# Two transformer blocks on one core: gate and MLA projections cut into pieces between attention steps, values in two passes with a fold, first stage reordered over four banks

## What is computed

```python
for l in range(DEPTH):
    xn = rms_norm(x, attn_norm[l])
    (nsa_q, kv_c, kv_s, kv_w, nsa_g, cq, ckv, k_rope_raw,
     gate_a, gate_b) = split_cols(xn @ w_in[l])
    o_a = nsa_attention(nsa_q, kv_c, kv_s, kv_w, nsa_g, cmp_pe[l], cmp_w1[l], cmp_w2[l], pos)
    o_b = mla_attention(cq, ckv, k_rope_raw, mla_q_norm[l], mla_kv_norm[l],
                        mla_w_uq[l], mla_w_ukv[l], pos)
    merged = (jax.nn.sigmoid(gate_a) * (o_a @ nsa_w_o[l])
              + jax.nn.sigmoid(gate_b) * (o_b @ mla_w_o[l]))
    x = x + merged @ w_out[l]
    hn = rms_norm(x, mlp_norm[l])
    x = x + jnp.square(jax.nn.relu(hn @ w_up[l])) @ w_down[l]
return rms_norm(x, final_norm)
```

## Time and profile before

| | |
|---|---|
| timed executions | 1684.75, 1685.53 and 1688.5 us; median 1685.53 us |
| span of the profiled execution, first to last instruction | 1683.2 us |
| busy share of the span, by engine | PE 94%, PE weight loads 77%, DVE 58%, ACT 40%, POOL 23% |
| mean granted TensorE clock | 0.974 of full speed |

### The profile page before, as it was taken

How to read it: one execution, slowest core, us unless ns; L and a number is a source line. 1 busy time by engine, 2 the same in 40 slices (tenths; PEclk the granted TensorE clock), 3 DMA queues, 4 the chain that set the end, 5 groups by cost and what they waited for, 6 DMA issues and landing times.

```text
span 1683.2 us, 23737 instructions
## 1 busy us (share of the span) xinstructions
PE 1587.0 (94%) x7742; PEld 1302.3 (77%) x7742; DVE 968.4 (58%) x1514; ACT 669.9 (40%) x1233; POOL 382.6 (23%) x410
## 2 busy tenths in 40 slices
PE   6899999889999999999998999999899999999996
PEld 4678878777778888888877888777678788888885
DVE  6765668775664343434566656777756544434346
ACT  5244447664342221322333552776623322222232
POOL 3660024343001010101056400434520000001010
PEclk9999889989999999999999998999999999999998
DMA  4234410002423233232223443000053222323232
GB/s 159 94 125 144 152 45 14 14 26 90 143 83 109 90 100 100 87 100 100 91 87 111 134 154 103 26 14 26 14 170 105 82 100 94 100 89 102 96 98 102
DMA packets 43238, 154.51 MB, mean 92 GB/s; under 512 B 5280, under 2 KB 5280, under 8 KB 43136
## 3 DMA queue, kind: packets, MB, share of 16 engines
q1 hardware_dynamic: 37152, 133.19, 23.9%
q0 software_dynamic: 5408, 17.95, 3.0%
q10 hardware_dynamic: 576, 2.10, 0.3%
HBM read 142.73 MB, written 10.49 MB: 91 GB/s over the span
## 4 chain that ended last, share of the span: by engine, by line
PE 71%; issue 13%; DVE 10%; ACT 3%; POOL 2%; DMA 0%; DVEq 0%; ACTq 0%; POOLq 0%
PE G L1066 17%; PE G L1067 17%; PE G L1068 17%; PE T L1243 3%; DVE wsplit L672 2%; PE S L1226 2%; PE O L1066 2%; DVE area L677 2%; PE O L1068 2%; PE O L1067 2%; PE S L1066 2%; PE S L1068 2%; PE S L1067 2%; PE O L1174 1%; POOL F L335 1%
## 5 line engine op out<-in xcount | busy, mean ns | idle before, releaser
L1066 PE MATMUL G<-xg,wsplit 128*128 128x512 f32 x960 | 382.5, 398 | 41.0 <-DVE wsplit L672 28.6
L1067 PE MATMUL G<-xg,wsplit 128*128 128x512 f32 x960 | 377.8, 394 | 0.0
L1068 PE MATMUL G<-xg,wsplit 128*128 128x512 f32 x960 | 377.6, 393 | 0.0
L672 DVE TENSOR_TENSOR wsplit<-stage,wsplit 128x1024 fp32r<-128x1024 f32 x229 | 299.6, 1308 | 86.8 <-ACT wsplit L391 86.5
L391 ACT ACTIVATE wsplit<-stage 128x1024 fp32r<-128x1024 f32 x229 | 240.8, 1051 | 230.5 <-PE G L1068 220.3
L1066 PEld LDWEIGHTS G<-xg,wsplit 128*128 128x128 f32 x960 | 183.0, 191 | 89.3 <-issue 37.4
L1066 PE MATMUL G<-area,wsplit 128*128 128x512 f32 x640 | 249.4, 390 | 0.0
L1068 PE MATMUL G<-area,wsplit 128*128 128x512 f32 x640 | 249.0, 389 | 0.0
L1067 PE MATMUL G<-area,wsplit 128*128 128x512 f32 x640 | 249.0, 389 | 0.0
L380 POOL TENSOR_TENSOR F<-Y 128x512 f32<-128x512 f32 x64 | 66.6, 1040 | 660.3 <-DVE Y L1037 660.3
L1068 PEld LDWEIGHTS G<-xg,wsplit 128*128 128x128 f32 x960 | 182.6, 190 | 39.1
(11 more groups left out here) (214 smaller groups left out, 2389.2 us busy)
## 6 DMA issues: line engine op xcount, KB each, us to landing
stage<-units SPq DMA_DIRECT2D x250, 512.0 KB, 3.3
gates<-Y POOLq DMA_DIRECT2D x32, 256.0 KB, 2.4
F<-gates POOLq DMA_DIRECT2D x32, 256.0 KB, 3.0
x<-x_in ACTq DMA_DIRECT2D x4, 512.0 KB, 10.1
out<-F SPq DMA_DIRECT2D x6, 256.0 KB, 2.1
rope<-tables POOLq DMA_DIRECT2D x1, 768.0 KB, 9.3
out<-Y SPq DMA_DIRECT2D x2, 256.0 KB, 2.2
F<-cmasks POOLq DMA_DIRECT2D x1, 192.0 KB, 10.1
```

The lines of the kernel that those rows point to most:

```text
L672: dve.tensor_tensor(wslot(u)[:, 1, :], stage[:, s, :], wslot(u)[:, 0, :], ALU.subtract)\
L1066: pe.matmul(dst, a(0), b(0), start=first, stop=False, skip_group_check=check)
L1067: pe.matmul(dst, a(0), b(1), start=False, stop=False, skip_group_check=check)
L1068: return pe.matmul(dst, a(1), b(0), start=False, stop=last, skip_group_check=check)
```

## The change

Nine things are done; the rest of the diff follows from them.

1. The 16 GATE tiles and the first MLA unit leave the first stage and the fixed steps. They are cut into four pieces each (for a gate two slices, six matmuls of 512 columns; for MLA the queries of each head, the keys, the values), and `FILL` puts the pieces at the end of steps 1 to 59. The other three MLA units get their pieces at steps 57 + 8p and after. The compressed scores, the transposes of their weights and the mean squares of the latent vectors go into steps too.
2. The work that ACT, DVE and POOL have with these pieces stands behind the step's own maximum and exponential.
3. For units that are used in the steps, the rest of the weights is made by POOL, not by DVE. The rests of the MLA queries and keys (kpe) go to POOL as well.
4. `values` takes two passes: the stationary side holds the hi part of the values in 64 columns and the rest in the other 64, and is multiplied by the hi and by the lo probabilities. The bank then holds two halves that must be added. This fold is done per head and no more per pair: ACT copies the lower half out and rounds the upper one, DVE subtracts, POOL adds (`output_hi`, `output_lo`, `output_rest`).
5. The compressed branch is added per head (two matmuls of 512 columns for each of 8 heads, before three for each of 4 pairs).
6. The hidden units (W1) take two passes in the same way, with a copy and an add on ACT and DVE.
7. The first stage begins with KC and VC, interleaves W1 units with projections, and its tiles go around over four banks (G0, G1, T0, T1); so do the tiles of W_OUT and the MLP (G0, G1, O0, O1).
8. Reciprocals of sums are taken for two jobs at once, at every second step (`LAG_SUM` 2), and POOL scales two jobs one after the other. For MLA jobs its second factor is 1.0, where it was none.
9. `s_wlo` is two semaphores, one for each slot of `stage`, since two engines now raise it.

The core of the diff:

```diff
-PREFIX = [("Q", 0), ("GATE", 0), ("Q", 1), ("GATE", 1), ("Q", 2), ("GATE", 2), ("Q", 3), ("GATE", 3),
...
+PREFIX = [("KC", 0), ("VC", 0), ("Q", 0), ("Q", 1), ("Q", 2), ("W1", 0), ("Q", 3), ("W1", 1), ("KS", 0), ("W1", 2),
+          ("KW", 0), ("W1", 3), ("V", 0), ("W1", 4), ("V", 1), ("W1", 5), ("MISC", 0), ("W1", 6), ("CQ", 0), ("W1", 7),
+          ("CQ", 1), ("W2K", 0), ("CQ", 2), ("W2V", 0)]
+EARLY = 11
+DURING = [("GATE", i) for i in range(EARLY)] + [("MLA", 0)] + [("GATE", i) for i in range(EARLY, NGATE)]
+LATE = [("MLA", p) for p in range(1, PAIRS)]
...
-LAG_SUM, LAG_T, LAG_SPLIT, LAG_PV, LAG_O = 1, 3, 4, 6, 7
+LAG_SUM, LAG_T, LAG_SPLIT, LAG_PV, LAG_O = 2, 3, 4, 6, 7
...
+for small, at in ((("CS", 0), 0), (("CS", 1), 2), (("WT", 0), 8), (("CM", 0), 10), (("CM", 1), 13), (("WT", 1), 15)):
+    FILL[at].append((small, 0))
+for n in range(len(DURING) * PIECES):
+    at = 1 + n if n < 4 * PIECES else 17 + (n - 4 * PIECES) * 43 // ((len(DURING) - 4) * PIECES)
+    FILL[at].append((DURING[n // PIECES], n % PIECES))
+for p in range(1, PAIRS):
+    for piece, at in enumerate((57, 58, 59, 64)):
+        FILL[at + 8 * p].append((("MLA", p), piece))
...
+                def scale(j):
+                    pool.wait_ge(s_rsum, l * (NJ // 2) + (j // 2 + 1))
...
+                    pool.tensor_scalar(p, p, rsum[:, j % 8:j % 8 + 1], gt[:, qt, col:col + 1] if j < NSA_NJ else 1.0,
+                                       ALU.mult, ALU.mult).then_inc(s_scl, 1)
...
+                def output_rest(n, scaled):
...
+                    pool.tensor_tensor(o_place(n, 1), F[half_, 5 + 2 * (n % 2), :], F[half_, 4 + 2 * (n % 2), :], ALU.add)\
+                        .then_inc(s_olo, 1)
...
+                    for c in range(2):
+                        ins = pe.matmul(dst[:, kt * P:S], v, PT[:, slot, c, kt * S:(kt + 1) * S - kt * P],
+                                        start=opens and c == 0, stop=closes(j) is not None and c == 1,
+                                        skip_group_check=True)
...
+                for i in range(STEPS):
+                    if i < NJ:
+                        scores(i)
+                    if 0 <= i - LAG_PV < NJ:
+                        values(i - LAG_PV)
+                    if 0 <= i - LAG_T < NJ:
+                        turn(i - LAG_T)
+                    for piece in FILL[i]:
+                        between(*piece)
```

1253 lines of the change are left out of this document (685 added, 568 removed), and 3 rows, old and new, of the table PREFIX.

## The result

The changed kernel takes 1734.46 us (median of 4 runs, 1731.96 to 1736.37) against 1685.14 us of the kernel before beside it (1684.68 to 1688.5): the ratio is 1.0281, 95% interval 1.0269 to 1.0293. The forecast was 1631 us. The profiled execution has a span of 1732.7 us and a mean granted clock of 0.951, where the kernel before had 1683.2 and 0.974.

What follows compares the result with a forecast made beforehand. PE bounds the NSA steps, a chain through engines the MLA steps; layers of 361 (115 + 177 + 58 + 11) and 357 us, 718 for 772.5, give a span of 1628.7 and a median of 1631 us, range 1592 to 1663.

Steps and rivals of the forecast that it cites:

- All three have room, so the pieces hide the waits; I add 4 us for the first dozen steps.: NSA steps: ACT, DVE and POOL have time to spare beside PE; 177 us a layer, with 4 us of waits.
- The values' term: NSA steps: each values pass removed saves PE some 0.16 us over the four widths, from 1.219 to 1.06 a step.
- So a third goes at the lone price, and about 9 remains.: First stage: POOL's rotation covers 6.7 us of DVE's list for a tile, which then takes about 9 us.
- the forecast's 9.8: First stage: DVE's list for one tile with POOL beside all of it, 9.8 us against 6.4 for PE.
- Rival 3: First stage fully serial on DVE and POOL, 128 and 125 us in the two layers, kernel 1657 us; chance 0.10.
- the forecast's 115: First layer's first stage: PE's 95 us, 16 for six tiles over PE's pace, 4 for the compression's blocks.
- The maximum no longer stands behind MLA work.: MLA steps: DVE's maximum, for which ACT's exponentials waited 24.2 us, would no longer be late; only scalings could be.
- The term of 58 us: First layer's MLA steps: PE's 53.4 us and 4.6 for late scalings by POOL; bounds 54 and 75.
- rival 4: NSA steps: POOL's queue of rests holds up the attention steps, 2 us a unit, kernel 1699 us; chance 0.06.
- rival 5: NSA steps: ACT's table loads hide behind nothing, 4 us more a layer, kernel 1639 us; chance 0.08.
- The dearer price: ACT's table loads: 2.66 us each with the engine drained, 10.6 for four, kernel at 1650 us; taken was 1.283 each.
- I leave them as they are: Output projections, W_OUT, MLP, start and end: 910.7 us, unchanged, at one 512-column matmul per 0.2273 us.

Runs made afterwards that it cites:

- e6: Changed kernel with compressed-branch small items in the outputs' banks, mean squares and transposes in earlier steps, gates alternating over the other two banks: 1693.65 us.
- e9: e6 with the second values pass issued twice in every step, so three passes, outputs not the reference's: 1709.03 us.
- e3: Changed kernel with POOL's products by the sines cut to 32 of 512 columns, outputs not the reference's: 1695.31 us.
- e7: Changed kernel with the rotation's exchange of halves as four copies on ACT and its product by the sines on DVE, none on POOL: 1701.19 us.
- m5: e6 and e7 together, with ACT, DVE and POOL work on MLA units' tiles after the table product cut to 32 of 512 columns: 1645.84 us.
- m6: m5 with reciprocals and scalings taken job by job: 1646.35 us.
- e2: Changed kernel with reciprocals and scalings taken one job at a time, one step after the exponential: 1733.88 us.
- e12: e7 and e8 together, with pieces of MLA units 1 to 3 in every second step, on even steps: 1701.11 us.
- e4: Changed kernel with all 68 pieces in steps 17 to 59 over both banks, and the second transpose of compressed weights at step 17: 1759.89 us.
- e8: e6 with six of the sixteen gates back in the first stage and the ten others spread over steps 1 to 59: 1684.1 us.
- e5: Changed kernel with DVE's rests of the MLA keys and values one step later: 1754.33 us.

## Why the prediction was wrong

The span is 1732.7 us for 1628.7 forecast, 104 us more. By its own terms: first stages 129.1 and 124.3 for 115 and 112 (26 us), NSA steps 199.3 and 200.8 for 177 (46), MLA steps 68.5 and 70.4 for 58 and 57 (24), tails 12.2 and 12.4 for 11 (3), all the rest 915.7 for 910.7 (5). Each part was on the same side. Slower than before was among the rivals, at 1699 us, but by POOL's rests in the NSA steps, which is not what happened.

**"All three have room, so the pieces hide the waits; I add 4 us for the first dozen steps."** This is the step that failed most. Busy shares of ACT, DVE and POOL said nothing on PE's own order: the small items went through one bank and the first four gates through another, and 11.4 of PE's 12.6 idle us are waits at the head of its queue for DVE to empty one of the two. With the clock that fell it cost 18 and 19 us in the two layers (71.6 and 72.9 for 53.5 and 53.6 in e6), not 4: 10.5 us of it in idle time, 7.6 in the same matmuls at a lower clock. With other banks and steps for these items (e6) the forecast's sum for these steps holds: 17 times 1.06, four gates of 5.45, 7.5 to 10.2 of scores and the 4 us make 51 to 54. In steps 17 to 63 it was nearly right as it stood: 47 times 1.06, twelve gates, an MLA unit and twelve matmuls of the compressed branch are 123 us, measured 127.3 and, in e6, 125.4; clock 1.0, and every wait short. The values' term was a little large, 0.13 us a pass for 0.16 (e9).

**"So a third goes at the lone price, and about 9 remains."** The first stage's mechanism was right, and its size was off. A tile without work on the blocks takes 9.9 us, not 9: POOL's products got longer themselves (a mean of 1.872 us for 1.669), so they lie beside nearly every operation of DVE. That is the forecast's 9.8 with nothing at the lone price, though two terms in it cancel: the add (L822), put at 0.7, takes 1.75, and the two query rests, put at 3.3, take 2.35. e3 and e7 show that it is POOL beside DVE and not DVE's own list, since e7 gives DVE one product more and the tile takes 8.4 instead of 11.1. The 7.7 us for which PE stands ahead of the first W1 unit, which the forecast did not have as a wait, are for the most part the same thing, 1.5 in e7 and 0.3 in e3. Rival 3, fully serial, had 128, and 129.1 was measured; but one us more a tile makes only 6 of the 14 us between the forecast and the first layer's stage. A term for the clock was missing. PE's idle time, 24 us, is close to the 23 in the forecast's 115 (20 of waits and 3 in the start). Its busy time is 105 us where the sum had 92 (95 without the 3 idle ones), at a clock of 0.91, and 97.5 in e7 at 0.98. How much of this would vanish behind DVE's list at full clock, no run shows.

The Trainium skill (SBUF — State Buffer, section "SBUF: two separate sides") has the shared ports as an exclusive lock for a whole instruction. The trace agrees in this: the time added does not grow with the operation, 1.07 us on 0.69 (L822) and on 1.23 (L767). I had taken a value between the bounds where the tiles had the upper one.

**"The maximum no longer stands behind MLA work."** It does. The work was moved behind the step's own maximum and exponential, which is ahead of the next step's. In the changed kernel, on DVE at the key tile of a unit (timeline in the MLA steps):

```profile
370.92 1.39 DVE L991 TENSOR_TENSOR area<-G,area 64x512 fp32r<-64x512 f32 x2 [1.27 <-ACT area L644]
372.34 0.56 DVE L963 TENSOR_REDUCE nmx<-S 128x1 f32<-128x384 f32 x1
372.81 0.55 DVE L973 TENSOR_TENSOR area_b<-T,area_b 128x384 fp32r<-128x384 f32 x1
```

DVE waits 1.27 us for ACT's copies (L644), makes the rests, and only then takes the maximum. The same wait stood in the kernel before, and is nearly unchanged:

```profile
PE T L1243 <- DVE area_b L727: 7.3, 4, 2.4
```

The term of 58 us needed PE at 53.4 with 4.6 of waits. PE's 53.4 was right (54.6 in m5, 54.1 in m6), the waits were 10, and 4 to 7 went to the lower clock. The 4.6 was for POOL's scalings, and PE does wait 3.6 us for them; what the forecast put at nothing is the wait for DVE, 6.6 us. The form with 1.0 takes 0.690 us, so the ungated price played no part, and e2 shows that without pairs the wait for DVE takes the place of the wait for POOL.

**Costs that were right or small.** POOL's rest of 1024 columns takes 2.39 us, inside 2.1 to 3.6 and near the 2.6 taken. The bounds of POOL's queue (rival 4) did not show in the NSA steps, where PE's longest wait for a scaling is 1.2 us up to step 16; the same mechanism did cost 12 us a layer when e12 moved the rest ahead of a pair. Table loads (rival 5) stand where they were put, four a layer. No run here isolates them, but in e6 PE's waits in steps 0 to 16, where they lie, are 2.0 us in all. The dearer price that the forecast names beside its own, with the engine drained at each switch, does not show. In the changed kernel a load starts 0.02 us after the instruction before it has ended, and ACT goes on at once behind it:

```profile
188.70 0.19 ACT L613 ACTIVATION_READ_ACCUMULATOR F<-S,nmx 128x1 f32 x1
188.91 1.28 ACT L553 ACT_TABLE_LOAD   x1
190.20 0.69 ACT L553 ACTIVATE E<-G,small 128x512 f32<-128x512 f32 x1
```

"I leave them as they are" held for the rest of the kernel but for 5 us: the output projections begin at a lowered clock (0.95 and 0.94) and take 46.9 and 47.3 us for 44.9.

**The comparison with before.** The change took 16 gates from a stage where PE was busy for 202 of 216 us. The forecast saw that the NSA steps have idle time to fill, which is right (e4, e8). For the stage that lost them it counted DVE's list too cheap, and it took no price for the clock, though the earlier trace rows show 0.90 in the MLA steps beside waits of the same kind. What remains open: how much of e6 is the banks and how much the steps; which of the units' copies and rests could be moved so that the MLA steps come near 61 us with the work done; and how much of e8's 10 us is cover and how much clock.

## What to carry to other kernels

Before work is put between steps of a bound engine, list what each piece waits for when it gets to the head of that engine's queue, bank by bank; busy shares of the others say nothing about it. When cover is taken from a stage, cost the other engines' lists there at the price that they have beside each other, not alone. "Behind this step's work" is ahead of the next step's: a wait is moved out of the way only if nothing critical follows it in the queue within its length.

## What the runs showed of the hardware

Idle time of PE costs more than itself. Between the MLA steps of the changed kernel and of e5 the idle time differs by 2.6 us and the stretch by 11.5, at clocks of 0.93 and 0.81. In the same steps of e12 PE is idle for 16.1 us, more than the 12.7 of e5, at a clock of 0.87. So the sum of the waits alone does not set the clock. The longest wait in these steps of the changed kernel is 2.5 us, and still the clock is below 1.

A DVE operation of two inputs from SBUF in the middle of POOL's products takes 1.07 us more whether it is 0.69 or 1.23 us long; the first one of a tile can get off with 0.25 to 0.48 more (L767: 1.47 to 1.70 us). POOL's 32x512 product takes 1.28 us where DVE is idle and 2.17 beside it. Scalings from PSUM (L804) stay at 0.68 us. Four copies of the same size on ACT, beside which DVE's operations keep their lone price, and one more product on DVE are 2.7 us a tile cheaper.

A table load takes 1.28 us on ACT, and the next instruction starts 1.29 us after the load's start.
